# Hybrid decoder trunk on one core: each mixer layer and its output pass in one program

## What is computed

```
for layer in range(2):
    hn = rms_norm(x, mix_pre_norm[layer])
    if layer % 2 == 0:
        m = gated_deltanet_mixer(hn, ...)   # 8 heads of 128; ends with
    else:
        m = gla_mixer(hn, ...)              # 4 heads of 256; ends with
        # o = rms_norm(o, o_gain) * silu(z)     by head
        # return o @ w_out                      (1024 x 1024) @ (1024 x 1024)
    x = x + rms_norm(m, mix_post_norm[layer])
    f = conv_glu_ffn(rms_norm(x, ffn_pre_norm[layer]), ...)
    x = x + rms_norm(f, ffn_post_norm[layer])
```

## Time and profile before

| | us |
|---|---|
| median of 3 runs | 3053.87 |
| the runs | 3619.89, 3053.87, 3048.57 |
| the profiled execution | 3050.12 |
| its span, first to last instruction | 3048.4 |
| TensorE busy | 2762.6 (91%) |
| VectorE busy | 1563.2 (51%) |
| ScalarE busy | 866.6 (28%) |
| GpSimd busy | 779.0 (26%) |

### The profile page before, as it was taken

The page is one execution under the profiler, slowest core; times in us unless marked ns, Lnnn a source line. Parts: engine busy times, 40 slices in busy tenths (PEclk is TensorE's granted clock), DMA queues, the critical chain, the costliest instruction groups (busy, mean ns, idle before and its releaser), DMA issues. The chain is left out here.

```text
span 3048.4 us, 35919 instructions
## 1 busy us (share of the span) xinstructions
PE 2762.6 (91%) x13277; PEld 2296.6 (75%) x13277; DVE 1563.2 (51%) x1780; ACT 866.6 (28%) x1213; POOL 779.0 (26%) x372
## 2 busy tenths in 40 slices
PE   7789898888597999999998599999688999999996
PEld 5677777777576888888887487788576888888885
DVE  4455545555234454544455675567354454444555
ACT  5244444344332111111111334333332111111112
POOL 2333223332142222222222211111232222222223
PEclk8799999999798999999999799999898999999998
DMA  2010110010242111111111310110332111111112
GB/s 106 21 42 28 34 41 34 28 41 7 71 151 83 49 48 48 48 41 55 48 48 48 119 35 31 46 48 34 130 119 77 49 41 48 55 48 48 48 62 97
DMA packets 62892, 172.11 MB, mean 56 GB/s; under 512 B 6177, under 2 KB 23137, under 8 KB 62833
## 3 DMA queue, kind: packets, MB, share of 16 engines
q1 hardware_dynamic: 62832, 171.33, 16.5%
HBM read 146.11 MB, written 25.20 MB: 56 GB/s over the span
## 5 line engine op out<-in xcount | busy, mean ns | idle before, releaser
L151 POOL TENSOR_TENSOR f_wlo<-f_raw,f_whi 128x1024 fp32r<-128x1024 f32 x132 | 335.6, 2551 | 1082.8 <-ACT f_whi L171 1082.8
L61 PE MATMUL f_up<-x_hi,f_whi 128*128 128x512 f32 x1408 | 550.4, 391 | 23.0 <-POOL f_wlo L151 23.0
L62 PE MATMUL f_up<-x_lo,f_whi 128*128 128x512 f32 x1408 | 549.7, 390 | 0.0
L63 PE MATMUL f_up<-x_hi,f_wlo 128*128 128x512 f32 x1408 | 549.6, 390 | 0.0
L171 ACT ACTIVATE f_whi<-f_raw 128x1024 fp32r<-128x1024 f32 x132 | 139.8, 1059 | 935.5 <-PE f_up L63 505.9
L61 PEld LDWEIGHTS f_up<-x_hi,f_whi 128*128 128x128 f32 x1408 | 265.6, 189 | 79.1 <-POOL f_wlo L151 23.8
L62 PEld LDWEIGHTS f_up<-x_lo,f_whi 128*128 128x128 f32 x1408 | 265.7, 189 | 55.3
L63 PEld LDWEIGHTS f_up<-x_hi,f_wlo 128*128 128x128 f32 x1408 | 265.4, 189 | 55.5
L61 PE MATMUL f_down<-f_whi,f_hhi 128*128 128x512 f32 x704 | 277.2, 394 | 17.5 <-issue 16.0
L211 DVE TENSOR_TENSOR acc<-f_down,acc 128x512 f32<-128x512 f32 x320 | 217.1, 689 | 123.2 <-PE f_down L63 120.3
L62 PE MATMUL f_down<-f_wlo,f_hhi 128*128 128x512 f32 x704 | 276.3, 392 | 0.0
(11 more groups left out here) (356 smaller groups left out, 4809.6 us busy)
## 6 DMA issues: line engine op xcount, KB each, us to landing
f_raw<-in_ffn_w_up SPq DMA_DIRECT2D x88, 512.0 KB, 3.2
f_raw<-in_ffn_w_down SPq DMA_DIRECT2D x44, 512.0 KB, 3.2
g_raw<-in_gdn_w_in SPq DMA_DIRECT2D x32, 512.0 KB, 3.5
l_raw<-in_gla_w_in SPq DMA_DIRECT2D x26, 512.0 KB, 3.3
after_ffn_xt<-x_mid SPq DMA_DIRECT2D x16, 512.0 KB, 4.1
first_xt<-in_x SPq DMA_DIRECT2D x8, 512.0 KB, 8.1
g_columns<-cum_rows SPq DMA_DIRECT2D x8, 512.0 KB, 3.8
mixed<-g_zc SPq DMA_DIRECT2D x8, 512.0 KB, 2.9
```

The lines of the kernel that those rows point to most:

```text
L61: pe.matmul(out, w_hi, x_hi, start=first, stop=False)
L62: pe.matmul(out, w_hi, x_lo, start=False, stop=False)
L63: return pe.matmul(out, w_lo, x_hi, start=False, stop=last)
L151: pool.tensor_tensor(w_lo[k][:, :], raw[k][:, :], w_hi[k][:, :].bitcast(F32), ALU.subtract) \
```

## The change

Each mixer's program now holds its output pass too (mixer_tail, which gives every engine its piece), and token_pass is used behind the feed-forward layers only. Nothing is left out of the computation.

The eight tiles of w_out are loaded and split into the places of tiles that the last head no longer needs (homes), and the token tiles of the finished heads (early = 7 of 8 rows of tiles in gdn, 6 of 8 in gla) are read from mixed into the place of x_lo (x_raw) and split into x_hi and x_lo, as soon as the last projection is over. The last head does not go to DRAM: its gated output zc or og is split from SBUF. GpSimd makes all low parts of the weights and of these tiles.

TensorE forms the products of the finished heads ("parts"): a unit is one product3 of one weight tile, half a row of tiles long (128x512). There are 70 units in gdn (7 weight tiles, 2 halves, 5 token tiles) and 36 in gla (6, 2, 3). Sums of the first E token tiles (4 in gdn, 2 in gla) are copied by ScalarE into SBUF ("keep", tiles acc), the next one stays in PSUM. In gdn 28 units stand in the last scan, 14 between it and output_turn, 28 behind that. In gla 12 stand behind the scan and 24 behind output_turn. Then "late" adds the last head's product for these tiles, VectorE adds the kept sum, and the remaining tiles (3 in gdn, 5 in gla) have all their products. The rest of the pass is as before, with a transpose behind a half of a tile instead of behind a whole one. gla's last head is written out, without the two loads beyond the end.

```diff
+def mixer_tail(nc, sem, eps, ident, w_out, mixed, x_in, x_out, post_gain, pre_gain, x_hi, x_lo, x_raw, early, w_hi, w_lo, w_raw,
+               acc, rows, scratch, part_ps, late_ps, turned):
...
+    def m_ps(t):
+        return part_ps if t >= E and (t - E) % 2 == 0 else late_ps
+
+    def m_of(t):
+        return acc[t] if t < E else m_ps(t)[:, :]
...
+        def keep(act, t, half):
+            act.wait_ge(s_part, 2 * t + half + 1)
+            act.activation(acc[t][:, halves(half)], part_ps[:, halves(half)], ACT.Copy).then_inc(s_kept, 1)
...
+            def m_deviation(t):
+                act.wait_ge(*((s_add, 2 * t + 2) if t < E else (s_m, t + 1)))
+                if t >= 2:
+                    act.wait_ge(s_xout[t % 2], 16 * (t // 2))
+                    act.wait_ge(s_xs, t - 1)
+                act.activation(xn[t % 2], m_of(t), ACT.Square, accum_out=ss[:, t:t + 1])
+                act.drain()
+                act.activation(std[:, t:t + 1], ss[:, t:t + 1], ACT.Sqrt, scale=1.0 / D,
+                               bias=eps[:, 0:1]).then_inc(s_mstd, 1)
...
+            for t in range(NT + 2):
+                if t < NT:
+                    m_deviation(t)
+                if 0 <= t - 1 < NT:
+                    x_deviation(t - 1)
+                if t >= 2:
+                    x_high(t - 2)
...
+        def passes(pool):
+            for t in range(NT):
+                pool.wait_ge(s_post, t + 1)
+                pool.wait_ge(s_xin[t % 2], 16 * (t // 2) + 16)
+                pool.tensor_tensor(xn[t % 2], xn[t % 2], xt[t % 2], ALU.add).then_inc(s_xn, 1)
...
+            def add(t):
+                dve.wait_ge(s_m, t + 1)
+                for half in range(2):
+                    dve.tensor_tensor(acc[t][:, halves(half)], late_ps[:, halves(half)], acc[t][:, halves(half)],
+                                      ALU.add).then_inc(s_add, 1)
+
+            def m_normed(t):
+                dve.wait_ge(s_mstd, t + 1)
+                dve.reciprocal(rms[:, t:t + 1], std[:, t:t + 1])
+                dve.drain()
+                dve.scalar_tensor_tensor(out=xn[t % 2], in0=m_of(t), scalar=rms[:, t:t + 1], in1=post,
+                                         op0=ALU.mult, op1=ALU.mult).then_inc(s_post, 1)
...
+            dve.wait_ge(s_kept, 2 * E)
+            add(0)
+            dve.wait_ge(s_gain, 32)
+            for t in range(NT + 2):
+                if t + 1 < E:
+                    add(t + 1)
+                if t < NT:
+                    m_normed(t)
+                if 0 <= t - 1 < NT:
+                    x_normed(t - 1)
+                if t >= 2:
+                    x_low(t - 2)
...
+        def parts(pe, some):
+
+            for n in some:
+                t, half, kt = n // (2 * early), n // early % 2, n % early
+                if t == 0 and half == 0:
+                    pe.wait_ge(s_wlo, kt + 1)
+                if kt == 0:
+                    pe.wait_ge(s_olo, t + 1)
+                    if t:
+                        pe.wait_ge(s_kept, 2 * t - 1 + half)
+                last = Tensor.product(pe, part_ps, t, half, kt, kt == 0, t < E and kt == early - 1)
+                if t < E and kt == early - 1:
+                    last.then_inc(s_part, 1)
+
+        @staticmethod
+        def late(pe, t, half):
+
+            for kt in range(early, KT):
+                last = Tensor.product(pe, m_ps(t), t, half, kt, t < E and kt == early, kt == KT - 1)
+            if half:
+                last.then_inc(s_m, 1)
+
+        @staticmethod
+        def passes(pe):
+            def turn(t):
+                pe.wait_ge(s_xs, t + 1)
+                if t >= 2:
+                    pe.wait_ge(s_free, t - 1)
+                for kt in range(KT):
+                    last = pe.transpose(turned[t % 2][:, kt, :], xs[t % 2][:, kt * P:(kt + 1) * P], ident[:, :])
+                last.then_inc(s_turn, 1)
+
+            pe.wait_ge(s_wlo, KT)
+            for t in range(E + 1):
+                pe.wait_ge(s_llo, (KT - early) * (1 if t < NT // 2 else 2))
+                if 1 <= t < E:
+                    pe.wait_ge(s_add, 2 * t)
+                for half in range(2):
+                    Tensor.late(pe, t, half)
+            turned_tiles = 0
+            for t in range(E + 1, NT):
+                pe.wait_ge(s_olo, t + 1)
+                if t == E + 1:
+                    pe.wait_ge(s_add, 2 * E)
+                else:
+                    pe.wait_ge(s_post, t - 1)
+                for half in range(2):
+                    for kt in range(early):
+                        Tensor.product(pe, m_ps(t), t, half, kt, kt == 0, False)
+                    Tensor.late(pe, t, half)
+                    if turned_tiles <= t - 2:
+                        turn(turned_tiles)
+                        turned_tiles += 1
+            for t in range(turned_tiles, NT):
+                turn(t)
...
+            def after(h):
+
+                free = [((s_a, halves(L, 1, 1)),), ((s_dx, 2 * H),), ((s_conv, 3 * L + 2),),
+                        ((s_t, 2 * J * L + 2), (s_qd, H)), ((s_conv, 3 * L + 3), (s_a, halves(L, 2, 1)))]
+                for kt_, waits in enumerate(free):
+                    for s, count in waits:
+                        sp.wait_ge(s, count)
+                    SyncTail.weight(sp, kt_)
+                sp.wait_ge(s_ost, 16 * L)
+                SyncTail.mixed_tile(sp, 0)
+                SyncTail.weight(sp, 5)
+                sp.wait_ge(s_m1p, 2 * J * H)
+                SyncTail.weight(sp, 6)
+                SyncTail.mixed_tile(sp, 1)
+                sp.wait_ge(s_g, H)
+                SyncTail.weight(sp, 7)
+                for t in range(2, NT):
+                    SyncTail.mixed_tile(sp, t)
+                sp.wait_ge(s_kdp, 8 * H)
+                sp.wait_ge(s_oT, H)
+                SyncTail.passes(sp)
...
+                if final(h):
+                    PoolTail.weight(pool, 0)
                 pool.tensor_tensor(kb[:, :, :], kt[:, :, :], wide(hg[:, G_CUM_EXP, :]), ALU.mult).then_inc(s_kb, 1)
...
+            def tail_beside():
+                return {0: lambda: ScalarTail.weight(act, 5),
+                        1: lambda: (ScalarTail.weight(act, 6), ScalarTail.mixed_tile(act, 1)),
+                        2: lambda: (ScalarTail.weight(act, 7), ScalarTail.mixed_tile(act, 2)),
+                        3: lambda: ScalarTail.keep(act, 0, 0),
+                        4: lambda: ScalarTail.mixed_tile(act, 3),
+                        5: lambda: ScalarTail.keep(act, 0, 1),
+                        6: lambda: ScalarTail.mixed_tile(act, 4),
+                        7: lambda: ScalarTail.keep(act, 1, 0)}
+
             def scan(h, projects, scans):
-                beside = {}
+                beside = {} if projects else tail_beside()
...
+            def after(h):
+                scan(h, False, True)
+                output_copy(h - 1)
+                output_squares(h - 1)
+                ScalarTail.keep(act, 1, 1)
+                output_deviation(h - 1)
+                output_norm(h - 1)
+                ScalarTail.keep(act, 2, 0)
+                ScalarTail.mixed_tile(act, 5)
+                ScalarTail.keep(act, 2, 1)
+                ScalarTail.mixed_tile(act, 6)
+                ScalarTail.keep(act, 3, 0)
+                for half in range(2):
+                    act.wait_ge(s_og, h + half)
+                    ScalarTail.last_high(act, zc, L, half)
+                    if half == 0:
+                        ScalarTail.keep(act, 3, 1)
+                ScalarTail.mixed_tile(act, 7)
+                ScalarTail.passes(act)
...
+                pe.wait_ge(s_u, halves(L, 2, 1))
                 for n in range(NT):
                     scan_value(h - 1, n)
+                    if n:
+                        TensorTail.parts(pe, range(4 * n - 4, 4 * n - 2))
                     scan_output(h - 1, n)
+                    if n:
+                        TensorTail.parts(pe, range(4 * n - 2, 4 * n))
+                done = 4 * NT - 4
+                pe.wait_ge(s_oc, h)
+                TensorTail.parts(pe, range(done, done + 14))
                 output_turn(h - 1)
+                TensorTail.parts(pe, range(done + 14, TensorTail.units))
+                TensorTail.passes(pe)
...
+                pe.wait_ge(s_u, HALVES * h)
+                TensorTail.parts(pe, range(0, 12))
                 output_turn(h - 1)
+                TensorTail.parts(pe, range(12, TensorTail.units))
+                pe.wait_ge(s_state, 7 * h)
+                TensorTail.passes(pe)
...
-        gdn(nc, consts, gdn_w_in, gdn_w_gates, gdn_conv_w, gdn_a_log, gdn_dt_bias, gdn_o_gain, x_hi, x_lo, mixed,
-            cum_rows)
-        token_pass(nc, "after_gdn", consts, x, x_mid[0], mix_post[0:1, :], ffn_pre[0:1, :], x_hi, x_lo,
-                   mixed=mixed, w_out=gdn_w_out)
+        gdn(nc, consts, gdn_w_in, gdn_w_gates, gdn_conv_w, gdn_a_log, gdn_dt_bias, gdn_o_gain, x_hi, x_lo, x_raw,
```

(6 more changed lines are left out.)

306 lines of the change are left out of this document (281 added, 25 removed).

## The result

The changed kernel takes 3015.52 us (median of 4, 3014.01 to 3017.27), the kernel before on the same chip 3053.85 (median of 4). The ratio is 0.9884, with a 95% interval of 0.9868 to 0.9899: 1.2% faster and clear of 1, though less than 2%; 38.3 us lie between the medians, where 3014 and -1.3% were forecast. The profiled execution took 3014.01, with a span of 3012.3, against 3050.12 and 3048.4. Run once more in a later series, the same kernel had 3010.37 beside 3050.09, ratio 0.9868 (0.9852 to 0.9883). So 5 us between two series are within what such runs scatter; where the text speaks of a few microseconds, it goes by stages of the profiles, which repeat better. The series ran on different chips, so times of two series are compared by their ratio to the kernel before.

A forecast was written before the change was run, and what follows sets the result against it. Nearly empty TensorE stretches, 51.2 us, between scans and separate output passes were the room. GDN's 17 us plus GLA's 20 off 3050.1 gave 3013, stated as 3014 (-1.3%); forecast range 3004 to 3022, eight in ten 2996 to 3034.

The forecast's parts named there:

- Scan with 28 units (1): GDN's last scan, filled with 28 units of output products: 29.8 us plus 1.5 for the lower clock, ending at 821.7.
- The wait for the output's copy (2): Behind GDN's scan: TensorE waits 1.3 us for the copy of the output and its signal.
- Parts behind the scan (3): GDN: 14 units 9.5 us, transposes 1.0, 28 units 19.1, ending at 852.6; the norm is covered.
- Late products (4): GDN, paced by VectorE's adds and norms: 16.3 us with 6.8 of TensorE work; tile 5 may start at 868.9.
- Tiles 5 to 7 (5 to 8): GDN's whole tiles: 13.0, 13.0 and 12.0 us, 4.6 of waiting before tile 6, and 1.5 for the clock falling.
- Tail (9): GDN's end, from the last product: 13.6 us, unchanged in kind.
- Clears (10): Semaphores cleared at program end: 1.5 us back in GDN, taking 0.1 each for 22 a queue instead of 5; GLA 1.1.
- The rule on the port pair: Norm of m with two SBUF inputs may be held by GpSimd: at most 3 us, in the range, not the forecast.
- (A): Rival: GpSimd's add and norm of x fall apart, no lock paid; 2998 us; chance 0.17, in full or part.
- (B): Rival: ScalarE's queue bounds the scan, each step waiting 1 to 2 us; 3026 to 3035; chance 0.20 together with (D).
- (C): Rival: loads do not run ahead and the kernel gets slower, 3084 at 5 us late each; chance 0.08 with anything above.
- (D): Rival: first units wait for weight splits until the scan's end, gaining about 10 us each; 3030; chance 0.20 with (B).

The follow-up runs named there:

- e2: Changed kernel with GDN's 28 units of output products moved from between the scan's steps to behind the last scan; 3019.09 us, ratio 0.9898.
- e7: Changed kernel with, in GDN, squares and norm of m of tiles 3 and 4 before the splits, fourth add before the first norm of x; 3008.88 us.
- e10: Changed kernel with e3's wait, e7's order, last tile's sum on VectorE in both passes, and GDN's squares of m written to their own place; 2993.02 us.
- e1: Changed kernel with only GDN's pass merged; GLA and its pass are those of the kernel before; 3033.92 us, ratio 0.9948.
- e5: Changed kernel with every semaphore cleared three times instead of once at the end of both merged programs; 3024.43 us, ratio 0.9909.
- e3: Changed kernel with GpSimd's sum of tiles 1 to 6 waiting for the previous tile's norm of x, both passes; 3005.63 us, ratio 0.9852.
- e4: Changed kernel with both transposes behind a whole later tile instead of in its middle, both passes; 3020.38 us, ratio 0.9893.
- after: Profile of the changed kernel itself, with no further edit; profiled execution 3014.01 us.
- c_after_again: The changed kernel run once more, unedited, in a later series; 3010.37 us, ratio 0.9868 to the kernel before.

## Why the prediction was right

The time and the sum of each layer were right, and so was the mechanism: products beside the scan and the norm, then a list on VectorE. Some of the exactness is luck, as terms that were off made up for each other. Its steps, in its order:

- **Scan with 28 units (1).** 29.8 and 1.5 for the clock were predicted, 31.3; from the first product to the end of the 28th unit it is 31.1. A step takes 3.90 us for 3.83, because a product starts every 0.232 us here and not every 0.227, of which more below. The chunk in which the clock rises takes 5.31, so the clock costs 1.4 there. One reading was off: of the 0.36 us that the prediction calls idle behind the state product, most is a third product, which its rows leave out:

```profile
796.80 0.39 PE L1569 MATMUL g_pt<-g_state,g_qdT 128*128 128x128 f32 x2
```

- **The wait for the output's copy (2).** 1.3 was put; it is nothing, since the last two units stand behind the last output and cover the copy (in e2, without them, it is 1.11).
- **Parts behind the scan (3).** 29.6 was put, measured 30.1. Expected to end at 852.6; the first late product starts at 852.73. That the two agree to 0.1 is luck: the scan began 0.9 later than before's, and the stretch from there was 1 us shorter than forecast.
- **Late products (4).** 16.3 us on VectorE from there, and tile 5 at 868.9; measured 868.68. Of gaps I had forecast 5 to 8 us before tile 5 (and 16.3 less 6.8, which is 9.5, in the sum); they come to 8.1 in all, but as three of 1.5 and one of 3.5. The norm of x and GpSimd's sum go as forecast (3.39 and 2.38 us), though the first norm of x took 2.79. The fourth add indeed stood behind it, which is what e7 takes away.
- **Tiles 5 to 7 (5 to 8).** Tile 6 at 886.5, measured 887.62; last product 913.0, measured 914.7. The wait of 4.4 was forecast as 4.6, by a chain that was only one of two (e7, e10). The clock is the one term of note that was too small. From 868.68 to 914.72 are 46.04 us, without the wait 41.6, where my three tiles at full clock make 38.0: 3.6 us, and I had allowed 1.5. Rows of both starts after a wait are at the lower level, and the mean over the three tiles is 0.89. e10 is the check: there no product of the three tiles is at the lower level, and without its wait they take 38.1. How far the clock falls behind a wait is not settled by the wait alone: behind the same 3.5 us before tile 5 there are 7 products at the lower level in the changed kernel, 8 in e1 and none in e2.
- **Tail (9).** 13.6 predicted, 13.65 measured.
- **Clears (10).** 1.5 predicted (17 at the 0.1 that I took are 1.7), 2.0 measured in GDN, and 1.1 against 1.3 in GLA: a clear is 0.12 us (e5).
- **GDN's sum** was -18.4 and 1.5 back. From the scan's first product it is -17.5 and 2.0 back; the next program's first product comes 15.4 us sooner behind the scan's start (163.17 before, 147.75 after). On the span's time it is 14.5, as the scan began 0.9 later. The missing 1.5 of 16.9 are the clock in tiles 5 to 7 (2.1 too little, of which the shorter stretch up to tile 5 gave 1.4 back), 0.5 of clears, and 0.2 by which the scan's first product stood behind the 790.4 that I counted from.
- **GLA's sum** was -20; it is -20.2 from the copy l_kt to the first product behind (159.84 to 139.61). The waits at the transposes were put at 2.6 and 0.35 in tile 3 and at 1.5 in each of tiles 5, 6 and 7, 7.5 us in all; they are 1.63 in tile 3 and 1.11 in each of the three, 5.0 in all. Most of the difference is lost again in the pace of the products, the units and the late ones, so the sum is right in part by chance. e3 and e4 show what the waits cost: 6.0 and 5.1 us.
- **The pace of a product**, which neither the forecast nor the change allows for. At full clock a product of the separate passes starts every 0.227 us and one of the merged passes every 0.232; in e1 GDN's merged pass has 0.232 and GLA's separate one 0.227 in the same profile. That is 1.9 us for the 384 products of a mixer, 3.8 in all. What sets it (where the operands lie is what differs) was not tested. It does not show in the sums because the transposes were put at their modelled length, 1.04, where the next product starts 0.79 behind their start: the two errors are of about one size.
- **What I cost at nothing** cost nothing: weight splits on ScalarE and GpSimd, twelve pieces to load. But the margin was not the one I gave. The weights take 6.3 and 5.9 us to land, the token tiles 8.1 and 7.5, against the 5.1 and 5.8 of before. The loads moved 312 GB/s around GLA's scan and 266 in the 12 us ahead of GDN's, where I had reckoned with the 149 that the old pass happened to move, which is no limit. So a load took longer than assumed, and more of them ran at once.
- **The rule on the port pair.** The forecast left the norm of m without a stretch. In after it has 1.70 once in GDN and 3.17 once in GLA, the rest 1.28: 2.3 us in all, within the 3 allowed.

**The rivals.** (A), no lock paid, did not come by itself, but e3 makes it: it was priced at 3 us in GDN and 8 in GLA, and gives 2.3 and 6.0. (B), ScalarE's queue as the bound of the scan, is out: from the second step on ScalarE waits 1.7 to 3.2 us for each product and copies the new value 0.03 us behind its end, as in the third step:

```profile
799.65 0.39 PE L1927 MATMUL g_pt<-g_state,g_wTn 128*128 128x128 f32 x2
...
800.07 0.28 ACT L1450 ACTIVATE g_vn<-g_pt 128x128 f32<-128x128 f32 x1 [2.41 <-PE g_pt L1927]
```

I was to be wrong if such a copy came over 0.5 us late, if the scan took over 33 us (31.1) or if the late stretch of GDN was under 10 us (15.9); none holds. Of the other signs, GLA's stretch is 129 us for 130, and the first output product stands at 795.2, not at 793: the scan began later and at the lower level. (C) and (D) are out with (B). The 1 us late start of GDN's scan, which I took at first for a sign of (B), is scatter (e1, c_after_again).

## What to carry to other kernels

Where a program ends with a serial tail and the next begins with loads, put the part of the next product that is already computable beside the tail, and count what is left as a list on the engine that finishes it: here the waits for VectorE outside the tails were 19.0 us, and 11.4 of them were the order of its list, the length of one instruction and one scratch tile. Before a wait is put down to one chain, look for a second of nearly the same length, above all through scratch tiles whose contents nobody reads. A shared port is avoided by one wait on a semaphore, if the instruction that is held back has slack; look then where the held instruction lands, for in e10 GpSimd's sum meets two norms of m instead, which take 3.5 us for 1.3. And the 13 us at the first product of each feed-forward layer are a boundary of the same kind as the one that this change took out, still open.

## What the runs showed of the hardware

**The port pair takes sides by operand.** In e10 GpSimd's sum starts 0.02 us before a norm of m three times. Twice m is a kept sum in SBUF, once it is in PSUM (g_pa); the gain is in SBUF each time:

```profile
869.04 2.40 POOL L957 TENSOR_TENSOR g_m<-g_m,g_vb 128x1024 f32<-128x1024 f32 x1 [3.90 <-issue]
869.06 3.47 DVE L980 SCALAR_TENSOR_TENSOR g_wTn<-g_decay,g_rms,g_kn 128x1024 f32<-128x1024 f32 x1
...
880.86 2.37 POOL L957 TENSOR_TENSOR g_m<-g_m,g_vb 128x1024 f32<-128x1024 f32 x1 [3.78 <-DVE g_inv L987]
880.88 1.28 DVE L980 SCALAR_TENSOR_TENSOR g_wTn<-g_pa,g_rms,g_kn 128x1024 f32<-128x1024 f32 x1
```

The same instruction takes 3.47 us with both inputs in SBUF (3.46 in the other such case) and 1.28 with one in PSUM. The longer one ends at 872.53, 1.09 us behind the end of GpSimd's: so it is held until that is over and then runs; it is not slowed all along. The Trainium skill (SBUF — State Buffer, "SBUF: two separate sides") says just this: the pair is an exclusive lock and no split of bandwidth, a VectorE instruction with two SBUF inputs needs it beside a GpSimd one that reads SBUF, and whoever starts first keeps it for the whole instruction. The runs agree, with a pair that starts 0.02 us apart, but for one detail: the held instruction ends 1.09 us behind, not the 1.28 that it takes alone. GpSimd's sums with x never pay (2.34 to 2.41 us), since each was first. Where VectorE was first, GpSimd pays: in after, in front of GLA's last scan, a GpSimd split takes 3.38 us where the one ahead of it takes 2.41. VectorE's product with two SBUF inputs had started at 2118.72, was held by that first split until 2120.18, and ended at 2121.27; only then could the second split go on.

```profile
2118.72 2.55 DVE L2511 TENSOR_TENSOR l_attn<-l_attn,l_tmp 128x1024 f32<-128x1024 f32 x1
...
2120.14 3.38 POOL L940 TENSOR_TENSOR l_outlo<-l_outraw,l_outhi 128x1024 fp32r<-128x1024 f32 x1
```

**A semaphore's clear is 0.12 us of its queue,** and nothing hides it at a program's end: at that price the 22 and 16 clears for a queue here are 2.6 and 1.9 us (an estimate from e5's two differences).
